# The last two projection tiles in halves: second halves between attention's first steps, and one selection tile later

## The chip, the cores and the metric

The kernel runs on one core of one Trainium2 chip. The metric is the device time of one execution in microseconds (us). TensorE (PE) multiplies matrices and transposes, VectorE (DVE), ScalarE (ACT) and GpSimd (POOL) compute on tiles, and SyncE (SP) issues the transfers between DRAM and on-chip memory (SBUF). Matmul results land in eight banks of PSUM.

## The reference

One decoder block on 1024 tokens of width 1024. Eight heads of width 64 attend with an index-based selection of 256 keys (DSA), and eight with a forgetting bias (FoX). Cut to what matters:

```
h = modulate(rms_norm(x), sh1, sc1)
proj = h @ w_in                      # q, k, v of both head groups, index heads, forget gates
q_d, k_d, v_d, iq, ik, iw, q_f, k_f, v_f, f_logit = split(proj)
score = sum_h(relu(iq . ik) * iw)    # per query and key, causal
keys = top_k(score, 256)             # the selection of the DSA heads
o_d = softmax(q_d . k_d over keys) @ v_d
o_f = softmax(q_f . k_f + cum_q - cum_k, causal) @ v_f
x = x + g1 * (concat(rms_norm(o_d), rms_norm(o_f)) @ w_out)
x = x + g2 * swiglu(modulate(rms_norm(x), sh2, sc2))
out = rms_norm(x)
```

## The kernel before

Every engine has its own program, written out in order. They meet in semaphores (`wait_ge`, `then_inc`), and an engine that waits holds up all that stands behind the wait in its program.

**Projections.** `w_in` is taken in seven chunks of columns (NC = 7), each in eight tiles of 128 tokens (TT = 8). A tile adds eight steps of k, each with three matmuls (function `three`, lines 2151 to 2153, since a number is kept as a high and a low part), into one PSUM bank: 24 matmuls of 128x512. The banks 0 to 3 are used in turn. ScalarE empties a tile into `stage` (line 1132), and SyncE stores it into DRAM (line 696). Chunk 6, the last, holds V of the DSA heads.

**Selection.** While the projections run, VectorE and ScalarE find for each tile of queries the threshold of the 256th key. `choose` (lines 1724 to 1747) then turns one tile of scores into a mask in eight steps on VectorE, for the tiles 2 to 7 in order. `advance(CHOICE_EARLY)` does the first five tiles, 2 to 6, before attention, and `CHOICE_LATE` puts the eight steps of tile 7 one by one behind steps of heads 1 and 2. Masks are used from head 8 on.

**Attention.** It runs over 128 steps s = 8 x head + tile. At step s TensorE computes the logits (lines 2330 and 2332), two matmuls for each group of up to 512 keys, into the banks 0 and 1 or 2 and 3. VectorE adds the bias and takes the maximum (`biased`, line 1798), ScalarE exponentiates (line 1251), TensorE transposes the probabilities two steps later (line 2311, banks 4 and 5), ScalarE copies them out, and the products with V (line 2357, banks 6 and 7) begin at step 12. FoX heads come first (0 to 7), then DSA heads.

**The head loop.** Heads need K and Q rows, which were stored in DRAM. There is one pair of buffers, `Qd` and `Kd`. GpSimd's `prepare(hd)` (lines 923 to 931) waits for their arrival, makes high and low parts in five instructions, and ends with line 931. SyncE's `load_qk(hd)` issues four fetches (line 663), and waits first until the head before is prepared:

```
def load_qk(hd):
    if hd >= 1:
        sp.wait_ge(k_lo, hd)
        sp.wait_ge(q_lo, hd)
```

After the last store of the projections SyncE's program reads, line 730 on:

```
for i in range(2):
    sp.wait_ge(stage_out[i], 16 * (NC - 1) * TT // 2)
sp.wait_ge(pj_pe, NC * TT)
sp.wait_ge(marks_free, 1)
load_values(0)
load_values(1)
for hd in range(2 * NH - 2):
    ...
    load_qk(hd + 2)
```

`stage_out` counts the landed stores of all tiles, `load_values` fetches V for a pair of heads (line 654, two fetches each). Heads 0 and 1 are fetched earlier, among the stores. On GpSimd `prepare(0)` runs under the projections, and `prepare(1)` waits for the end of all tiles (`pj_pe`), because its results lie where the low part of h was.

## Time and profile before

| | |
|---|---|
| time, median of 3 runs | 1386.51 us (1385.52 to 1388.21) |
| the profiled execution | 1386.66 us, of it span 1384.7 us |
| TensorE busy | 1313.3 us, 95% of the span |
| VectorE, ScalarE, GpSimd busy | 72%, 50%, 61% |
| projections' last tile emptied by ScalarE | 370.07 us after the span's start |
| heads 6 and 8 begin on TensorE | 454.87 and 485.94 us |

Times in the rows below are microseconds from the span's start. Each timeline row gives start, duration, engine, line of the program, instruction, the tile written and the tile read. A bracket gives the idle time of the engine before it and what ended it ("issue" where the profile shows nothing that it waited for). Matmuls overlap, so the distance of two starts is what one costs.

### The profile page before, as it was taken

Reading aid. Unit: us, or ns where it says so; the run is one execution under the profiler, and the core shown is the slowest. Engines: PE = TensorE matmul, PEld = TensorE weight load, DVE = VectorE, ACT = ScalarE, POOL = GpSimd, SP = SyncE. Lnnn points to the kernel's source line nnn. Section 1 sums busy time; section 2 is a strip of 40 time slices with the busy share of each in tenths; the row PEclk is TensorE's granted clock in tenths of the full one; section 3 lists DMA queues with packets and bytes.
Section 4 is the critical chain, followed back from the end, with each engine's and each line's share of the span. In section 5 each row is a group of like instructions: output and inputs, shape, how many; then the busy total and the mean of one; then the engine's idle time right before and its main releaser. Section 6 shows DMA issues by size and latency. Waiting matters only on the chain.

```text
span 1384.7 us, 19484 instructions
## 1 busy us (share of the span) xinstructions
PE 1313.3 (95%) x6595; PEld 1074.1 (78%) x6595; DVE 995.2 (72%) x1583; ACT 696.0 (50%) x1396; POOL 848.1 (61%) x552
## 2 busy tenths in 40 slices
PE   1999999999999999899999899999999999999996
PEld 0988778888777677668888788888888888788885
DVE  4563779999866888876569666555556666589998
ACT  6623345563388777773345344333444333454545
POOL 0161403324249745931027899888889984798995
PEclk9799999999999999999999999999999999999998
DMA  9131312342345777605010333233333234998873
GB/s 380 55 97 56 94 52 92 107 124 77 110 113 160 239 221 219 200 32 193 38 45 31 97 120 109 93 107 107 115 114 110 89 122 152 391 352 301 288 249 143
DMA packets 130379, 200.53 MB, mean 145 GB/s; under 512 B 10637, under 2 KB 65093, under 8 KB 129258
## 3 DMA queue, kind: packets, MB, share of 16 engines
q1 hardware_dynamic: 130282, 199.30, 43.1%
q8 instruction: 53, 0.87, 0.3%
q14 instruction: 44, 0.36, 0.1%
HBM read 156.99 MB, written 42.27 MB: 144 GB/s over the span
## 4 chain that ended last, share of the span: by engine, by line
PE 78%; DVE 9%; issue 4%; ACT 3%; DMA 3%; POOL 2%; SPq 1%; ACTq 0%; DVEq 0%; POOLq 0%
PE PS L2151 20%; PE PS L2152 20%; PE PS L2153 20%; PE PS L2357 4%; PE PS L2311 4%; DVE AS L2017 3%; PE PS L2330 2%; DMA ada<-in_ada_w_dram 2%; DVE BS L2022 1%; PE PS L2332 1%; POOL WSf L1012 1%; PE PS L2335 1%; ACT LP L1251 1%; DVE PS L2074 1%; POOL WS L1024 1%
## 5 line engine op out<-in xcount | busy, mean ns | idle before, releaser
L1330 ACT CAST WS<-WSf 128x512 fp32r<-128x512 f32 x110 | 68.5, 622 | 203.6 <-POOL WSf L1012 202.9
L1024 POOL TENSOR_TENSOR WS<-WSf,WS 128x512 fp32r<-128x512 f32 x109 | 163.4, 1506 | 4.4 <-ACT WS L1330 4.4
L1012 POOL TENSOR_TENSOR WSf<-rawg 128x512 f32<-128x512 f32 x55 | 78.5, 1428 | 117.0 <-PE PS L2153 112.5
L2151 PE MATMUL PS<-yh,WS 128*128 128x512 f32 (+2 forms) x360 | 140.4, 390 | 1.5 <-DVE yl L1931 1.5
L2152 PE MATMUL PS<-yl,WS 128*128 128x512 f32 (+2 forms) x360 | 140.1, 389 | 0.0
L2153 PE MATMUL PS<-yh,WS 128*128 128x512 f32 (+2 forms) x360 | 140.0, 389 | 0.0
L2151 PE MATMUL PS<-BS,AS 128*128 128x512 f32 x308 | 121.0, 393 | 4.6 <-DVE BS L2022 3.4
L2017 DVE TENSOR_TENSOR AS<-rawa,AS 128x512 fp32r<-128x512 f32 x77 | 104.9, 1382 | 23.0 <-ACT AS L1389 22.8
L2153 PE MATMUL PS<-BS,AS 128*128 128x512 f32 x308 | 120.5, 391 | 0.0
L2152 PE MATMUL PS<-BS,AS 128*128 128x512 f32 x308 | 120.4, 391 | 0.0
L1251 ACT ACTIVATE LP<-LP,nmin 128x128 f32<-128x128 f32 (+7 forms) x128 | 100.2, 783 | 23.3 <-DVE nmin L1798 22.0
L1043 POOL TENSOR_TENSOR BS<-rawb,BS 128x512 fp32r<-128x512 f32 x57 | 90.6, 1595 | 27.9 <-ACT BS L1393 27.7
L2151 PE MATMUL PS<-XH,WS 128*128 128x512 f32 x264 | 103.5, 392 | 4.0 <-POOL WS L1024 4.0
L1640 DVE TENSOR_SCALAR_CACHE_REDUCE marks_c<-sel,bis 128x640 f32<-128x640 f32 (+4 forms) x135 | 103.3, 818 | 0.6
L2153 PE MATMUL PS<-XH,WS 128*128 128x512 f32 x264 | 103.2, 391 | 0.0
L2152 PE MATMUL PS<-XL,WS 128*128 128x512 f32 x264 | 103.2, 391 | 0.0
L2311 PE MATMUL PS<-ident,LP 128*128 128x128 f32 x576 | 90.4, 282 | 6.8 <-ACT PTb L1241 2.7
L1036 POOL TENSOR_TENSOR rawb<-rawb 128x512 f32<-128x512 f32 x55 | 90.3, 1651 | 7.9 <-DMA rawb<-in_w_down_dram 7.9
L1157 ACT ACTIVATE PS<-sel,bis 128x896 f32<-128x896 f32 x64 | 67.6, 1056 | 50.3 <-DVE bis L1695 35.2
L2311 PEld LDWEIGHTS PS<-ident,LP 128*128 128x128 f32 x576 | 66.2, 143 | 29.0 <-ACT PTb L1241 8.7
L1012 POOL TENSOR_TENSOR WSf<-rawu 128x512 f32<-128x512 f32 x55 | 84.5, 1537 | 3.4 <-PE PS L2153 2.5
L1389 ACT CAST AS<-rawa 128x512 fp32r<-128x512 f32 x77 | 47.9, 622 | 75.0 <-PE PS L2153 64.2
(337 smaller groups left out, 3820.4 us busy)
## 6 DMA issues: line engine op xcount, KB each, us to landing
rawb<-in_w_down_dram SPq DMA_DIRECT2D x132, 256.0 KB, 4.5
rawa<-gu_scratch SPq DMA_DIRECT2D x77, 256.0 KB, 4.5
gu_scratch<-GS SPq DMA_DIRECT2D x55, 256.0 KB, 4.5
raw<-in_w_in_dram SPq DMA_DIRECT2D x24, 512.0 KB, 3.9
rawg<-in_w_gate_dram SPq DMA_DIRECT2D x22, 512.0 KB, 4.3
rawu<-in_w_up_dram SPq DMA_DIRECT2D x22, 512.0 KB, 4.3
ada<-in_ada_w_dram SPq DMA_DIRECT2D x8, 1024.0 KB, 15.3
qk_scratch<-stage SPq DMA_DIRECT2D x32, 256.0 KB, 2.1
```

The costliest lines, as they stand in the source:

```text
L1012: pool.tensor_tensor(WSf[m % N_SLOT][:], left(i, mat, a), left(i, mat, b), ALU.add if sign > 0 else ALU.subtract).then_inc(ws_sum, 1)
L1024: pool.tensor_tensor(lo, WSf[m % N_SLOT][:] if b else left(i, mat, a), hi.bitcast(F32), ALU.subtract).then_inc(ws_ready, 1)
L1036: pool.tensor_tensor(r[:, 0, :], r[:, 0, :], r[:, 1, :], ALU.add if RIGHT[DOWN[m // PAIRS]][2] > 0 else ALU.subtract).then_inc(gb_sum, 1)
L1043: pool.tensor_tensor(b[:, 1, :], rawb[m % DOWN_RAW_B][:, 0, :], b[:, 0, :].bitcast(F32), ALU.subtract).then_inc(gb_lo, 1)
L1251: act.activation(LP[:, u % 3, 0:n], LP[:, u % 3, 0:n], ACT.Exp, bias=nmin[:, u:u + 1], scale=-1.0, accum_out=sums[:, u:u + 1]).then_inc(ex ...
L1330: act.copy(WS[m % N_SLOT][:, 0], src).then_inc(ws_hi, 1)
L1640: did(dve.tensor_scalar(marks[0][:, n_tk % 2, 0:P * (t + 1)], view(t), limit, 0.0, op, ALU.add, accum_out=col(0, t)))
L2017: dve.tensor_tensor(AS[m % DOWN_SLOTS][:, 1, :], rawa[m % DOWN_RAW_A][:], AS[m % DOWN_SLOTS][:, 0, :].bitcast(F32), ALU.subtract).then_inc ...
L2151: pe.matmul(dst, left[0], right[0], start=first, stop=False)
L2152: pe.matmul(dst, left[0], right[1], start=False, stop=False)
L2153: return pe.matmul(dst, left[1], right[0], start=False, stop=last)
L2311: last = pe.transpose(dst[:, i * P:(i + 1) * P], src, ident[:])
```

## The change

The tiles 6 and 7 of chunk 6 (`HELD_TILES`) go into the banks 6 and 7. At their place in the projections TensorE does only the first half, k = 0 to 3, and counts it in `held_half`. The rest goes in four pieces of six matmuls behind the steps 0 to 3 of attention (`HELD_AT`). VectorE and not ScalarE copies the two tiles to `stage`, behind the bias steps 3 and 5 (`HELD_EVAC`). ScalarE makes a dummy exponential ahead of emptying tile 5. GpSimd's `prepare(1)` waits for `held_half`. `advance(CHOICE_EARLY)` does four tiles of selection, and the sixteen steps of tiles 6 and 7 stand behind steps of heads 1, 2 and 3.

```diff
-CHOICE_TILES = ((), (1, 2, 6, 7), (1, 2, 6, 7))
+CHOICE_TILES = ((), (1, 2, 3, 6, 7), (0, 1, 2, 5, 6, 7), (1, 2, 3, 6, 7))
...
-CHOICE_EARLY = 5 * CHOICE_OPS
+CHOICE_EARLY = 4 * CHOICE_OPS
+HELD_TILES = (TT - 2, TT - 1)
+HELD_AT = {0: (TT - 2, 4), 1: (TT - 2, 6), 2: (TT - 1, 4), 3: (TT - 1, 6)}
+HELD_EVAC = {3: TT - 2, 5: TT - 1}
...
+def proj_bank(ch, t):
+
+    return t if ch == NC - 1 and t in HELD_TILES else (TT * ch + t) % 4
...
             pool.wait_ge(cumT_ok, 2)
             prepare(0)
+            pool.wait_ge(held_half, len(HELD_TILES))
+            prepare(1)
             pool.wait_ge(pj_pe, NC * TT)
-            prepare(1)
...
                 elif step[0] == "tile":
+                    if step[1] == NC - 1 and step[2] in HELD_TILES:
+                        continue
+                    if step[1:] == (NC - 1, HELD_TILES[0] - 1):
+                        act.activation(junk[:, 0:1], ones[:, 0:1], ACT.Exp)
                     if step[3:] != (0,):
                         evac_tile(step[1], step[2])
...
-            dve.wait_ge(pj_pe, NC * TT)
+            def evac_held(t):
+                n = (NC - 2) * TT + t
+                dve.wait_ge(pj_pe, (NC - 1) * TT + t + 1)
+                dve.wait_ge(stage_out[n % 2], 16 * (n // 2))
+                dve.tensor_copy(stage[:, n % 2, :], PS[:, proj_bank(NC - 1, t), :]).then_inc(pj_ev, 1)
+
+            dve.wait_ge(held_half, len(HELD_TILES))
             for s in range(UNITS):
                 hd, t = divmod(s, TT)
                 biased(s)
+                if s in HELD_EVAC:
+                    evac_held(HELD_EVAC[s])
...
+                held = ch == NC - 1 and t in HELD_TILES
+                dst = PS[:, proj_bank(ch, t), 0:w]
+                if held and rows_of.start == 0:
+                    pe.wait_ge(sign_cnt, len(SIGN_TILES) * BISECT)
...
+                elif held and rows_of.stop == KT // 2:
+                    last.then_inc(held_half, 1)
...
-                    tile(*step[1:])
+                    if step[1] == NC - 1 and step[2] in HELD_TILES:
+                        tile(*step[1:], part=0)
+                    else:
+                        tile(*step[1:])
...
-                    pe.wait_ge(pj_ev, NC * TT - 2 * (1 - u))
+                    pe.wait_ge(pj_ev, NC * TT - len(HELD_TILES))
...
+                        if p == 0 and g == 0:
+                            pe.wait_ge(pj_ev, NC * TT)
...
                 values(s, 2)
+                if s in HELD_AT:
+                    t, k = HELD_AT[s]
+                    tile(NC - 1, t, rows_of=range(k, k + 2))
```

TensorE's order at the end of the projections, before the change (`wh`, `hh` and `hl` are weights and input of the projections, `KA` and `QT`, `CK` and `CQ` the two parts of the logits, and `LP` the probabilities that are transposed):

```order
L2151 MATMUL PS<-wh,hh 128x512
L2152 MATMUL PS<-wh,hh 128x512
L2153 MATMUL PS<-wh,hl 128x512
L2330 MATMUL PS<-KA,QT 128x128
L2332 MATMUL PS<-CK,CQ 128x128
L2330 MATMUL PS<-KA,QT 128x256
L2332 MATMUL PS<-CK,CQ 128x256
L2330 MATMUL PS<-KA,QT 128x384
L2332 MATMUL PS<-CK,CQ 128x384
L2311 MATMUL PS<-ident,LP 128x128
```

TensorE's order at the same place in the changed kernel, from the last matmul before attention:

```order
L2175 MATMUL PS<-wh,hl 128x512
L2361 MATMUL PS<-KA,QT 128x128
L2363 MATMUL PS<-CK,CQ 128x128
L2173 MATMUL PS<-wh,hh 128x512
L2174 MATMUL PS<-wh,hh 128x512
L2175 MATMUL PS<-wh,hl 128x512
L2173 MATMUL PS<-wh,hh 128x512
L2174 MATMUL PS<-wh,hh 128x512
L2175 MATMUL PS<-wh,hl 128x512
L2361 MATMUL PS<-KA,QT 128x256
L2363 MATMUL PS<-CK,CQ 128x256
```

Six projection matmuls now stand between the logits of step 0 and those of step 1; the same holds behind the steps 1, 2 and 3.

VectorE's order where selection ends and attention begins, before the change (`sel` is the scores and mask, `marks_c` a scratch tile, and the rows with `strip` and `nmin` are the bias steps 0 and 1):

```order
L1735 SCALAR_TENSOR_TENSOR marks_c<-marks_c 128x896
L1739 SCALAR_TENSOR_TENSOR marks_c<-marks_c,bis 128x896
L1743 SCALAR_TENSOR_TENSOR sel<-sel,bis,marks_c 128x896
L1747 TENSOR_SCALAR sel<-sel 128x896
L1798 ISA LP,nmin<-PS,strip 128x128
L1798 ISA nmin 128x1
L1798 ISA LP,nmin<-PS,strip 128x256
L1798 ISA nmin 128x1
```

VectorE's order in the changed kernel, from the bias step 3 to the bias step 6:

```order
L1812 ISA LP,nmin<-PS,strip 128x512
L1812 ISA nmin 128x1
L1864 COPY stage<-PS 128x512
L1812 ISA LP,nmin<-PS,strip 128x640
L1812 ISA nmin 128x1
L1812 ISA LP,nmin<-PS,strip 128x768
L1812 ISA nmin 128x1
L1864 COPY stage<-PS 128x512
L1812 ISA LP,nmin<-PS,strip 128x896
```

The steps of tile 6 (128x896) are gone from the place ahead of attention, and two copies into `stage` stand behind the bias steps 3 and 5. SyncE's and GpSimd's instructions stand in the same order as before.

## Rows read from the trace of the kernel before

**Rows 1.** The page: busy time of the engines, and the chain by engine

```profile
PE 1313.3 (95%) x6595; PEld 1074.1 (78%) x6595; DVE 995.2 (72%) x1583; ACT 696.0 (50%) x1396; POOL 848.1 (61%) x552
...
PE 78%; DVE 9%; issue 4%; ACT 3%; DMA 3%; POOL 2%; SPq 1%; ACTq 0%; DVEq 0%; POOLq 0%
```

**Rows 2.** ScalarE's timeline at the end of the projections: start us, us, instruction

```profile
364.63 0.60 ACT L1132 ACTIVATE stage<-PS 128x512 f32<-128x512 f32 x1 [4.84 <-PE PS L2153]
370.07 0.60 ACT L1132 ACTIVATE stage<-PS 128x512 f32<-128x512 f32 x1 [4.84 <-PE PS L2153]
370.69 1.28 ACT L1251 ACT_TABLE_LOAD   x1
```

**Rows 3.** TensorE's timeline at attention's first steps; in brackets the idle time before

```profile
369.88 0.22 PE L2330 MATMUL PS<-KA,QT 128*128 128x128 f32 x1
...
370.73 0.39 PE L2330 MATMUL PS<-KA,QT 128*128 128x256 f32 x1 [0.52 <-ACT stage L1132]
...
372.53 0.33 PE L2311 MATMUL PS<-ident,LP 128*128 128x128 f32 x1 [0.95 <-ACT LP L1251]
372.62 0.48 PE L2330 MATMUL PS<-KA,QT 128*128 128x512 f32 x1
...
395.01 0.33 PE L2330 MATMUL PS<-KA,QT 128*128 128x128 f32 x1
```

**Rows 4.** SyncE's queue after the projections (what it issues)

```profile
372.75 2.02 SPq L654 DMA_DIRECT2D Vn<-v_scratch  x4
378.03 1.09 SPq L663 DMA_DIRECT2D Qd<-qk_scratch  x2
...
392.94 1.11 SPq L663 DMA_DIRECT2D Qd<-qk_scratch  x2
```

**Rows 5.** GpSimd's timeline: in the preparation of heads 1, 2, 3 and 6

```profile
375.58 2.37 POOL L931 TENSOR_TENSOR QT<-Qd,QT 64x1024 fp32r<-64x1024 f32 x1
...
385.05 1.04 POOL L923 CAST QT<-Qd 128x1024 fp32r<-128x1024 f32 x1 [5.01 <-DMA Kd<-qk_scratch]
...
399.79 2.04 POOL L923 CAST QT<-Qd 128x1024 fp32r<-128x1024 f32 x1 [6.92 <-DMA Kd<-qk_scratch]
...
451.55 3.22 POOL L931 TENSOR_TENSOR QT<-Qd,QT 64x1024 fp32r<-64x1024 f32 x1
```

**Rows 6.** GpSimd's waits from 385 to 490 us: us in total, times, longest

```profile
POOL QT L923 <- DMA Kd<-qk_scratch: 27.2, 6, 7.0
```

**Rows 7.** SyncE's waits in the same stretch

```profile
SPq L660 <- POOL QT L931: 62.7, 7, 12.5
```

**Rows 8.** TensorE's timeline where heads 6 and 8 begin

```profile
454.87 0.30 PE L2330 MATMUL PS<-KA,QT 128*128 128x128 f32 x1 [2.74 <-issue]
...
485.94 0.30 PE L2330 MATMUL PS<-KA,QT 128*128 128x128 f32 x1 [0.81 <-issue]
```

**Rows 9.** Windows: engines' busy time, granted clock, DMA share, GB/s

```profile
373.50:378.50 5.00, 5.00 (x26) 4.54 (x25) 2.72 (x7) 3.90 (x11) 4.86 (x3) 0.66 0.71 210
394.00:398.50 4.50, 4.50 (x40) 3.40 (x37) 2.98 (x8) 3.56 (x9) 0.00 (x0) 1.00 0.94 235
```

**Rows 10.** DMA issues from 372 to 376 us: KB each, us to landing

```profile
Vn<-v_scratch SPq DMA_DIRECT2D x4, 256.0 KB, 3.5
```

**Rows 11.** DMA issues from 425.6 to 427 us, behind a head's rows

```profile
Vn<-v_scratch SPq DMA_DIRECT2D x2, 256.0 KB, 5.3
```

**Rows 12.** VectorE's timeline: selection of tile 6, one bias step, two later selection steps

```profile
361.34 0.68 DVE L1724 TENSOR_SCALAR sel<-sel,bis 128x896 f32<-128x896 f32 x1
...
368.45 0.63 DVE L1747 TENSOR_SCALAR sel<-sel 128x896 f32<-128x896 f32 x1
...
376.67 0.96 DVE L1798 CUSTOM_DVE_ANT_0 LP<-PS,strip 128x768 f32<-128x768 f32 x1 [1.11 <-PE PS L2332]
...
399.65 1.28 DVE L1739 SCALAR_TENSOR_TENSOR marks_d<-marks_d,bis 128x1024 f32<-128x1024 f32 x1
...
406.44 3.23 DVE L1743 SCALAR_TENSOR_TENSOR sel<-sel,bis,marks_d 128x1024 f32<-128x1024 f32 x1
```

More of the change, by code:

```diff
@@ L477, in build @@
         pj_ev = sem("pj_ev")
+        held_half = sem("held_half")
         ir_st = sem("ir_st")
@@ L2188, in tile @@
                     pe.wait_ge(mod1_ok, 2)
-                if q >= 4 and rows_of.start == 0:
+                held = ch == NC - 1 and t in HELD_TILES
+                dst = PS[:, proj_bank(ch, t), 0:w]
+                if held and rows_of.start == 0:
+                    pe.wait_ge(sign_cnt, len(SIGN_TILES) * BISECT)
+                elif q >= 4 and rows_of.start == 0:
                     pe.wait_ge(pj_ev, q - 3)
@@ L2201, in tile @@
                         rows = slice(half * BANK, (half + 1) * BANK)
-                        last = three(PS[:, q % 4, 0:w], (hi[:, cols], lo[:, cols]), (hh[:, k, rows], hl[:, k, rows]),
+                        last = three(dst, (hi[:, cols], lo[:, cols]), (hh[:, k, rows], hl[:, k, rows]),
                                      k == 0, k == KT - 1)
@@ L2206, in tile @@
                     rows = slice(t * P, (t + 1) * P)
-                    last = three(PS[:, q % 4, 0:w], (hh[:, k, rows], hl[:, k, rows]), (hi[:, cols], lo[:, cols]),
+                    last = three(dst, (hh[:, k, rows], hl[:, k, rows]), (hi[:, cols], lo[:, cols]),
                                  k == 0, k == KT - 1)
```

## Prediction

> **What bounds the kernel now.** I read the page first. TensorE is busy for 95% of the span and holds 78% of the chain that ended last [rows 1], so a change can gain only by taking time out of TensorE's path. The place to look at is the handover from the projections to attention. The timelines show what is spent there: after the last projection matmul TensorE starts attention at 369.88, stands 0.52 us until ScalarE has emptied the last tile, and 0.95 us until the first exponential is there [rows 3], which has a 1.28 us table load ahead of it [rows 2]. In the following 5 us the granted clock averages 0.66 [rows 9], so part of them ran at 1.2 GHz instead of 2.4.
>
> Then I asked whether a TensorE that is earlier there stays earlier. It does not have to. Each head needs its K and Q rows: SyncE fetches them from DRAM, GpSimd prepares them, and SyncE may fetch the next head's rows only when that is done, as there is one pair of buffers. SyncE issued head 2's fetch at 378.03 [rows 4], right when GpSimd ended head 1 (375.58 + 2.37 = 377.95 [rows 5]). GpSimd began on head 2 at 385.05, and the next fetch went out at 392.94 [rows 4, 5]. This loop has no slack: from 385 to 490 us GpSimd waited for the fetched rows six times [rows 6] and SyncE for GpSimd seven times [rows 7]. It takes 14.9 us in this round, and from 378.03 to the start of head 8 at 485.94 [rows 4, 8] 107.9 us for seven heads, 15.4 us each. TensorE alone goes faster: from head 2 (395.01 [rows 3]) to where it stands ready for head 6 (454.87 - 2.74 = 452.13 [rows 8]) it takes 57.1 us for four heads, 14.3 each. So it catches up with the loop. At head 6 it stands 2.74 us, until GpSimd has ended (451.55 + 3.22 = 454.77 [rows 5]), and at head 8 another 0.81 [rows 8]. **Up to head 8 the loop sets the time, and the loop hangs on the moment at which head 2's fetch is issued.**
>
> **The change, part by part.**
>
> *Half tiles moved on TensorE.* One projection tile of 24 matmuls takes 370.07 - 364.63 = 5.44 us [rows 2]. Two second halves are 24 matmuls too, so attention starts 5.44 us earlier, at 364.44. The matmuls themselves stay. They go where TensorE stood or waited for ScalarE, together with the 0.52 us of waiting for the last tile. The table load, now made by a dummy exponential before tile 5 is emptied, leaves the path: ScalarE waits 4.84 us for each tile [rows 2], which hides 1.28. That would be worth up to 0.52 + 0.95 + the slow clock's share, 0.34 x 5 = 1.7, some 3.2 us in all, if nothing else bound.
>
> *Selection of tile 6 on VectorE.* Its eight steps run from 361.34 to 368.45 + 0.63 = 369.08 [rows 12], 7.7 us. They would have been in the way of a bias step at 364.8, and now go into heads 1 to 3. There they cost TensorE nothing as long as what they delay is less than its standing at head 6, 2.74 us and more; without that cover they would cost up to 7.7 us.
>
> *Head 1's preparation on GpSimd.* It now waits for the two half tiles only, which end 5.44 us earlier, so it ends at 377.95 - 5.44 = 372.5. This looks like a gain for the loop, but nothing follows from it, because of the next part.
>
> *The last two stores on SyncE's queue.* Nothing in SyncE's program changes, but it is in order: store of tile 6, store of tile 7, wait for both to land, four fetches of V, and only then head 2's K and Q. Tile 7 used to be emptied at 370.07 + 0.60 = 370.67 [rows 2]. Now VectorE does it after the bias step of step 5. TensorE must do before it: four pieces, 5.44; the logits of steps 0 to 5, which are 2 x 128 x (1 + ... + 6) = 5376 columns at the projections' rate of 5.44 / (24 x 512) us, 2.38; and six transposes at about 0.1 (372.53 to 372.62 [rows 3]), 0.6. That is 8.4 us from 364.44, so 372.9. The bias step takes 0.96 [rows 12] with some 0.3 before it, and the copy is bounded by nothing and 0.6 (ScalarE's for the same tile [rows 2]); with 0.6 it ends at 374.8. From the emptied tile to the first fetch of V it took 372.75 - 370.67 = 2.08 us, and the four issues 2.02 [rows 2, 4]. So head 2's fetch goes out at 374.8 + 2.08 + 2.02 + 0.04 = 378.9 instead of 378.03: **about 0.9 us later**, though everything before it is earlier. Each wait of TensorE in its first five steps adds to this one to one.
>
> *K and Q behind V.* Before, V's 1 MB was done when K and Q were asked for (landing 3.5 us after issue [rows 10]). Now they are asked for directly behind it. If the transfers simply overlap, the fetch takes as long as before: added cost 0. If they queue, V's bytes flow until 3.5 us after its last issue at about 378.4, to 381.9, and then K and Q need 4.5 us more (the 394.0 to 398.5 window, DMA 94% busy [rows 9]) and about 1.3 to be noticed (398.5 to 399.79 [rows 5, 9]): 387.7, against 378.9 + 7.0 = 385.9. Added cost 1.8. A sign of queueing is that V issued directly behind K and Q takes 5.3 instead of 3.5 us [rows 10, 11]. I take 1.4, nearer to the upper end. The Trainium skill, page "DMA: Bandwidth & Descriptors", section "Queues, rings and completion order", says that each DMA engine consumes the descriptors of a ring in order; by that rule the cost is the full 1.8, and the sum below is 0.4 higher. Rows 10 and 11 agree with it.
>
> *GpSimd against VectorE.* GpSimd's cast of head 3 at 399.79 took 2.04 us instead of 1.04 [rows 5]; VectorE's selection step of 1.28 us had begun at 399.65 [rows 12]. Another such step took 3.23 us at 406.44 [rows 12]. The two delay each other, and each meeting can add up to 1 us to the loop. The change shifts the phases and puts eight more such steps into heads 1 to 3, so the loop may lose one meeting (-1.0) and get up to two (+2.0). I take 0. The Trainium skill, page "SBUF — State Buffer", section "Who interferes with whom", speaks against the change here: such VectorE steps and GpSimd's take a port in turn, for a whole instruction. By that rule each new meeting costs, and the two above agree with it in size.
>
> **Sum.** Loop later by 0.9 + 1.4 + 0 = 2.3 us at head 8. Head 2 begins at about 387.3 + (392.94 - 385.05) = 395.2, hardly later than before, after a stand of some 3 us; TensorE may then lose again what the slow clock took, 1.7 us, and reaches head 6 before the loop does. From head 8 on TensorE leads the time again, so the 2.3 stay. The profiled execution took 1386.66 us, 0.15 above the median of three runs; median: 1386.51 + 2.3 = **1388.8 us**. That is slower by 0.17%; a difference below 0.2%, 2.8 us, can't be told from none here.
>
> **The rivals.**
> - *The loop holds* (my forecast, 0.70). With the fetch alone +0.9 and one meeting lost, -0.1; with full queueing and two meetings, 0.9 + 1.8 + 2.0 = +4.7. Time 1386.4 to 1391.2, nearly symmetric about 1388.8. For it: rows 4 to 8.
> - *VectorE becomes the bound* (0.10). Its 7.7 us more in heads 1 to 3 hold up TensorE, by way of bias steps, for more than the 2.74 + 2.3 - 0.2 - 1.7 = 3.1 us that are there before head 6. If half of it, 3.9, and two steps lengthened by 2 us like that of 406.44 come through, 7.9 - 3.1 = 4.8 us are added to the 2.3: 1393.6. Against it: the steps stand behind bias steps and are short beside a head's 14 us.
> - *The ramp's gain is kept* (0.12). The 3.2 us are saved, and the loop is not late. That asks for a fetch of head 2 issued by 375, three us earlier than before; it decides from a tile 7 emptied by 370.8. Then 1386.5 - 3.2 = 1383.3. Against it stands that the copy of tile 7 has 8.4 us of TensorE before it, which start at 364.44. A smaller form is that K and Q do not hang behind V's issues and meetings are lost.
> - *Nothing moves* (0.08): the fetch goes out at 378.0, since steps 0 to 5 are shorter than I make them: 1386.5.
>
> **How the numbers follow.** The median is slower by over 2.8 us (above 1389.3) in 0.38 of the first case (0.27) and all of the second: 0.37. It is faster by as much (below 1383.7) in some 0.08 of the third and nowhere else: 0.08. The rest is 0.55. The range 1385.6 to 1391.4 takes in the bounds of the first case and the last one, and leaves out the second and most of the third.
>
> **What the profile would show.** The first attention matmul at 364.4; no table load before the first exponential; tile 7 copied by VectorE at about 374.2; V's fetches at 376.9 and head 2's at 378.9; GpSimd's cast of head 2 at 387.3 instead of 385.05; TensorE standing some 3 us before head 2; heads 6 and 8 beginning 2.3 us later than 454.87 and 485.94. I am wrong if head 2's fetch goes out before 378, if the six waits of GpSimd are gone, or if TensorE no longer stands at head 6.

## The result, and the profile after

The changed kernel took 1398.05 us in the median of four runs (1395.71 to 1398.89), the kernel before 1387.36 (1385.52 to 1389.32): ratio 1.0073, 95% interval 1.0052 to 1.0095. It is slower by 0.73%, about four times what was forecast, and outside the range. The profiled execution took 1397.99 us, 11.3 more than the one of before.

What was forecast up to the fetch of head 2 is there. ScalarE's timeline has the table load behind the last tile but one that it empties, not ahead of the first exponential [rows 2]:

```profile
352.60 0.60 ACT L1142 ACTIVATE stage<-PS 128x512 f32<-128x512 f32 x1 [4.84 <-PE PS L2175]
353.22 1.28 ACT L1202 ACT_TABLE_LOAD   x1
...
364.14 0.40 ACT L1265 ACTIVATE LP<-LP,nmin 128x128 f32<-128x128 f32 x1 [5.50 <-DVE nmin L1812]
```

VectorE's timeline has the two held tiles' copies, at 369.78 and 373.36, 0.69 us each:

```profile
369.78 0.69 DVE L1864 COPY stage<-PS 128x512 f32<-128x512 f32 x1
...
373.36 0.69 DVE L1864 COPY stage<-PS 128x512 f32<-128x512 f32 x1
```

SyncE's queue issues head 2's fetch (line 672) at 378.96 instead of 378.03 [rows 4], directly behind the four fetches of V, and the next one at 397.63 instead of 392.94:

```profile
370.50 3.90 SPq L705 DMA_DIRECT2D v_scratch<-stage  x2
376.12 2.74 SPq L663 DMA_DIRECT2D Vn<-v_scratch  x4
378.96 1.10 SPq L672 DMA_DIRECT2D Qd<-qk_scratch  x2
380.10 1.24 SPq L672 DMA_DIRECT2D Kd<-qk_scratch  x2
381.38 1.24 SPq L750 DMA_DIRECT2D RX<-qk_scratch  x2
...
397.63 1.11 SPq L672 DMA_DIRECT2D Qd<-qk_scratch  x2
```

TensorE's timeline starts attention at 363.28. It stands 6.87 us before head 2, and still 2.65 at head 6 and 0.83 at head 8, which start 9.1 and 9.2 us later than before [rows 8]:

```profile
363.28 0.22 PE L2361 MATMUL PS<-KA,QT 128*128 128x128 f32 x1
...
397.66 0.45 PE L2361 MATMUL PS<-KA,QT 128*128 128x128 f32 x1 [6.87 <-POOL QT L940]
...
424.20 0.51 PE L2361 MATMUL PS<-KA,QT 128*128 128x512 f32 x1 [1.29 <-DVE nmin L1812]
...
463.99 0.30 PE L2361 MATMUL PS<-KA,QT 128*128 128x128 f32 x1 [2.65 <-issue]
...
495.14 0.30 PE L2361 MATMUL PS<-KA,QT 128*128 128x128 f32 x1 [0.83 <-issue]
```

So nearly all of the time is lost between 378 and 495 us, in the loop of SyncE and GpSimd. Its legs, worked out from the two timelines: "fetch" runs from the issue of a head's Q rows to GpSimd's first cast of them (in heads 5 to 7 it holds parts of GpSimd's rotation of RX too), "prepare" from there to the end of its last instruction. The next issue follows 0.07 us later.

```
head      before: fetch, prepare    after: fetch, prepare    loop later by (with the 0.93 at its start)
2                 7.02  7.82               9.14  9.46              4.7
3                 6.85  8.80               7.62  8.15              4.8
4                 6.66  7.84               6.90 10.78              8.0
5                 7.27  8.68               8.60  8.67              9.3
6                 6.86  8.65               6.69  8.62              9.1
7                 6.79  9.37               6.98  9.20              9.1
8                 6.93  7.83               7.01  7.81              9.2
```

Three places hold nearly all of it: the fetch of head 2 (+2.1), and the preparations of heads 2 and 4 (+1.6 and +2.9) with the rotation ahead of head 5's (6.01 instead of 4.70 us). GpSimd's timeline shows what happened in them. An undisturbed cast takes 1.04 us, whether of 128 or of 64 partitions; here one takes 2.77, one 3.04 and one 2.02:

```profile
388.10 1.05 POOL L932 CAST QT<-Qd 128x1024 fp32r<-128x1024 f32 x1 [14.62 <-DMA Kd<-qk_scratch]
389.09 1.05 POOL L933 CAST KA<-Kd 128x1024 fp32r<-128x1024 f32 x1
390.07 2.77 POOL L935 CAST CQ<-Qd 64x1024 fp32r<-64x1024 f32 x1
...
420.37 1.04 POOL L932 CAST QT<-Qd 128x1024 fp32r<-128x1024 f32 x1 [6.98 <-DMA Kd<-qk_scratch]
421.35 3.04 POOL L933 CAST KA<-Kd 128x1024 fp32r<-128x1024 f32 x1
424.34 2.02 POOL L935 CAST CQ<-Qd 64x1024 fp32r<-64x1024 f32 x1
...
431.23 6.01 POOL L949 TENSOR_TENSOR RT<-RX,turnF 128x1024 f32<-128x1024 f32 x2
```

VectorE's timeline has a selection step beside each of them:

```profile
389.80 2.22 DVE L1749 TENSOR_TENSOR_SCAN marks_d<-marks_d 128x896 f32<-128x896 f32 x1
...
421.28 2.28 DVE L1749 TENSOR_TENSOR_SCAN marks_d<-marks_d 128x1024 f32<-128x1024 f32 x1
424.06 1.40 DVE L1753 SCALAR_TENSOR_TENSOR marks_d<-marks_d,bis 128x1024 f32<-128x1024 f32 x1
```

The scan of tile 7 has just begun when GpSimd reaches its second cast. It ends at 423.56, and the cast ends 0.83 us behind it, as if it had stood until then. The next cast ends 0.90 us behind the following step. Undisturbed, no other step is as long as the scan (2.02 us on 896 columns, 2.29 on 1024 in the kernel before), and the prediction's bound of one microsecond for a meeting came from a shorter step [rows 5, 12]. The Trainium skill, page "SBUF — State Buffer", section "Who interferes with whom", has a VectorE instruction with two inputs in SBUF contend with a GpSimd instruction that reads SBUF, and the one that comes second blocked for the whole of the other; these rows agree.

From the start of head 8 on TensorE to the end the two profiles differ by another 2.4 us (901.2 us instead of 898.8). That is not laid to the change: over all profiles of this study this stretch lies between 893.8 and 901.7.

The slow clock of attention's first steps [rows 9] is gone: windows of the changed kernel give a granted clock of 1.00 from 366 to 396 us. Behind the stand before head 2 it comes back. The columns are the length, the busy time of TensorE (its matmuls, its weight loads), VectorE, ScalarE and GpSimd, the granted clock, the DMA share and GB/s:

```profile
366.00:396.00 30.00, 22.74 (x148) 18.05 (x147) 16.83 (x36) 21.21 (x53) 15.16 (x10) 1.00 0.45 123
...
398.00:402.00 4.00, 4.00 (x19) 2.73 (x18) 2.86 (x6) 1.93 (x5) 0.00 (x0) 0.50 0.77 196
402.00:404.00 2.00, 2.00 (x13) 1.63 (x11) 0.00 (x0) 0.84 (x2) 0.00 (x0) 0.78 0.63 141
```

### The profile page after: what moved, and what is told of

The parts are those of the page before. It is cut to its first block, busy times and chain, and to the rows that moved or that the text cites. A ratio compares the mean times of both kernels' runs of the same rounds, so it can differ in the third digit from the quotient of the medians.

```text
span 1396.3 us, 19486 instructions
## 1 busy us (share of the span) xinstructions
PE 1315.9 (94%) x6595; PEld 1076.5 (77%) x6595; DVE 1007.5 (72%) x1585; ACT 695.4 (50%) x1395; POOL 845.8 (61%) x552
## 4 chain that ended last, share of the span: by engine, by line
PE 56%; DVE 5%; issue 4%; ACT 2%; POOL 2%; DMA 1%; SPq 0%; ACTq 0%; DVEq 0%; POOLq 0%
PE PS L2173 15%; PE PS L2175 15%; PE PS L2174 15%; PE PS L2390 4%; PE PS L2342 4%; PE PS L2361 2%; POOL WSf L1022 1%; DVE AS L2039 1%; PE PS L2366 1%; PE PS L2363 1%; DVE LP L1812 1%; POOL WS L1034 1%; PE PS L2407 0%; DMA rawa<-gu_scratch 0%; PE PS L2372 0%
## 5 line engine op out<-in xcount | busy, mean ns | idle before, releaser
L2039 DVE TENSOR_TENSOR AS<-rawa,AS 128x512 fp32r<-128x512 f32 x77 | 100.7, 1323 | 25.7 <-ACT AS L1403 25.5
L2361 PE MATMUL PS<-KA,QT 128*128 128x512 f32 (+1 forms) x192 | 78.2, 407 | 13.6 <-POOL QT L940 6.9
```

The costliest lines, as they stand in the source:

```text
L2039: dve.tensor_tensor(AS[m % DOWN_SLOTS][:, 1, :], rawa[m % DOWN_RAW_A][:], AS[m % DOWN_SLOTS][:, 0, :].bitcast(F32), ALU.subtract).then_inc ...
L2361: pe.matmul(dst, q, KA[i][:, b:b + w], start=True, stop=False)
```

## The experiments

Each was timed in turn with the kernel before on the same chip. All were made from the changed kernel, except where "from the kernel before" is said. "Head 8" is the end of its preparation in the profile (before 485.85, changed 495.04), "ratio" the time against the kernel before. A tenth of a per cent is 1.4 us. Medians of different rows can come from different chips, so they are compared by the ratios.

```
                                     median us   ratio [95% interval]         head 8
selection alone (from before)          1391.57   1.0027 [1.0002, 1.0053]      490.33
held tiles alone                       1397.25   1.0063 [1.0040, 1.0087]      497.49
fetch first                            1386.68   0.9994 [0.9967, 1.0020]      487.55
V then K and Q (from before)           1391.90   1.0028 [1.0001, 1.0055]      491.67
one column                             1390.30   1.0007 [0.9989, 1.0025]      489.42
fetch first, one column                1382.65   0.9961 [0.9942, 0.9981]      480.96
fetch first, RX later                  1386.37   0.9994 [0.9970, 1.0018]      484.01
the same, steps placed                 1387.98   0.9994 [0.9970, 1.0018]      484.76
scan and two-input steps short         1392.45   1.0028 [1.0011, 1.0046]      491.06
multiplications short                  1395.08   1.0048 [1.0030, 1.0066]      494.87
changed kernel again                   1397.05   1.0067 [1.0044, 1.0091]      495.55
fetch first, selection of before       1388.88   0.9993 [0.9977, 1.0010]      485.56
```

**The selection alone**, from the kernel before.

```diff
-CHOICE_TILES = ((), (1, 2, 6, 7), (1, 2, 6, 7))
+CHOICE_TILES = ((), (1, 2, 3, 6, 7), (0, 1, 2, 5, 6, 7), (1, 2, 3, 6, 7))
-CHOICE_EARLY = 5 * CHOICE_OPS
+CHOICE_EARLY = 4 * CHOICE_OPS
```

> The kernel before with the change's selection alone: four tiles ahead of attention, the sixteen steps of tiles 6 and 7 behind steps of heads 1 to 3; no held tiles. Theory (GpSimd's preparation loop sets the time, and selection steps on VectorE that fall into a preparation lengthen it): head 2's fetch goes out at 378.0 as before; the scan of head 3's part and the step behind it fall into the preparation of head 4, which takes 10 to 11 us instead of 7.8; head 8 begins 2 to 4 us later than 485.94; time 2 to 4 us above the kernel before. Rival (the ramp and the fetch order alone make the loss, selection costs nothing): within 1 us of the kernel before. Rival (VectorE holds up TensorE's bias steps): slower too, but with GpSimd's preparations at 7.8 us and TensorE's waits for VectorE grown.

The time is 3.7 us above the kernel before (0.3 to 7.4), and head 8 is 4.5 us later, although head 2's fetch goes out 2.5 us earlier, at 375.51, since the projections end earlier in this profile (why was not found). From that issue to the end of head 8's preparation the loop takes 114.8 us instead of 107.8. 2.2 of the 7.0 us are the preparation of head 4, which takes 10.01, with the end of tile 7's scan and the step after it beside its first two casts. So the new steps are paid for without any held tile.

Another 1.8 us are the fetch of head 2, which takes 8.79 instead of 7.02. V is not the reason: it is issued 5.3 us ahead of the fetch, as in the kernel before [rows 4].

```profile
370.19 2.02 SPq L654 DMA_DIRECT2D Vn<-v_scratch  x4
...
375.51 1.09 SPq L663 DMA_DIRECT2D Qd<-qk_scratch  x2
```

Where V stands directly ahead the Q rows land late, and here they do not. The DMA issues of head 2's rows (KB each, median us to landing), in the kernel before, with the selection alone, and in the changed kernel:

```profile
Qd<-qk_scratch SPq DMA_DIRECT2D x2, 256.0 KB, 3.9
Kd<-qk_scratch SPq DMA_DIRECT2D x2, 256.0 KB, 4.9
```

```profile
Qd<-qk_scratch SPq DMA_DIRECT2D x2, 256.0 KB, 3.9
Kd<-qk_scratch SPq DMA_DIRECT2D x2, 256.0 KB, 5.9
```

```profile
Qd<-qk_scratch SPq DMA_DIRECT2D x2, 256.0 KB, 5.2
Kd<-qk_scratch SPq DMA_DIRECT2D x2, 256.0 KB, 6.6
```

In all seven profiles with V directly ahead of head 2's fetch the Q rows take 5.1 to 5.8 us, in the seven others 3.6 to 4.0. The K rows behind them vary by more, and why is open.

**The held tiles alone**: the same two lines, set back in the changed kernel.

> The changed kernel with the selection of the kernel before: five tiles ahead of attention, eight steps in heads 1 and 2. The bias of step 0 then waits for VectorE until about 369. Theory: tile 7 is copied at about 376.7, head 2's fetch goes out at 380.8 (2.8 us later than 378.03), behind V, which adds 1.6 to 2.1; with 0 to 1 us of meetings the loop is 4.4 to 6 us late at head 8, time 4 to 6 us above the kernel before. Rival (selection steps are the whole loss): time within 1 us of the kernel before. Rival (the ramp's gain shows once selection is out of the way): 2 to 3 us below the kernel before.

As slow as the whole change, but by another way. Tile 6's selection now stands between TensorE's first logits and VectorE's first bias step (370.37), and head 1's preparation, brought forward to 363.77, falls beside it and takes 11.00 us. TensorE waits 3.8 us for that step, and its granted clock is 0.50 from 370 to 376, while it works on the second halves that the stores wait for. Head 2's fetch goes out at 385.05, 7 us later than before and 4 later than I expected, and takes 10.28. The time is 8.7 us above the kernel before, more than the 4 to 6 of the theory. The costs of the two parts do not add up: each shifts where the other's work falls.

**Fetch first**: head 2's K and Q are issued ahead of the held tiles' stores, when head 1's preparation is done.

```diff
                     q = TT * (ch - 1) + t
+                    if (ch, t) == (NC - 1, HELD_TILES[0]):
+                        load_qk(2)
                     sp.wait_ge(pj_ev, TT * ch + t + 1)
...
-                load_qk(hd + 2)
+                if hd >= 1:
+                    load_qk(hd + 2)
```

> The changed kernel with head 2's K and Q fetch issued ahead of the stores of the two held tiles. Theory: the fetch goes out at 372.6 instead of 378.96, lands in 7 us, GpSimd ends head 2 at 387 to 388 instead of 397.56, and TensorE does not stand at head 2. The loop then leads by some 6 us over the kernel before, loses 2 to 5 in meetings with selection, and head 6 begins at 450 to 454 against 454.87 before: time 1 to 4 us below the kernel before, 11 to 14 below the changed one. Rival (the late fetch is not what costs; VectorE's load is): TensorE gains at head 2 but is held up in heads 1 to 3, and the time stays more than 5 us above the kernel before.

SyncE's queue and GpSimd's timeline:

```profile
371.81 1.08 SPq L672 DMA_DIRECT2D Qd<-qk_scratch  x2
372.93 1.24 SPq L672 DMA_DIRECT2D Kd<-qk_scratch  x2
374.21 1.06 SPq L707 DMA_DIRECT2D v_scratch<-stage  x2
380.18 2.02 SPq L663 DMA_DIRECT2D Vn<-v_scratch  x4
382.24 1.21 SPq L752 DMA_DIRECT2D RX<-qk_scratch  x2
...
387.26 1.11 SPq L672 DMA_DIRECT2D Qd<-qk_scratch  x2
```

```profile
379.14 1.30 POOL L935 CAST QT<-Qd 128x1024 fp32r<-128x1024 f32 x1 [5.32 <-DMA Kd<-qk_scratch]
...
396.91 1.04 POOL L935 CAST QT<-Qd 128x1024 fp32r<-128x1024 f32 x1 [9.72 <-DMA Kd<-qk_scratch]
...
414.33 3.10 POOL L938 CAST CQ<-Qd 64x1024 fp32r<-64x1024 f32 x1
417.39 3.34 POOL L941 TENSOR_TENSOR CK<-Kd,KA 64x1024 fp32r<-64x1024 f32 x1
```

The fetch is 7.15 us earlier than in the changed kernel and takes 7.33 us with V behind it and not ahead. The time falls back to that of the kernel before, and not to the 1 to 4 us below it that I expected: head 8 is 7.5 us earlier than in the changed kernel and still 1.7 later than before. The queue is now in front of head 3's fetch, which has V and RX ahead of it and takes 9.65, and head 4's preparation meets scan and next step again (11.14). V itself is now late, issued at 380.18 instead of 372.75, and TensorE's timeline has a wait for it:

```profile
384.01 0.40 PE L2393 MATMUL PS<-PTa,Vn 128*64 128x256 f32 x1 [1.20 <-DMA Vn<-v_scratch]
```

**V, then K and Q**, from the kernel before: V is only asked for when head 1 is prepared, so that head 2's fetch stands directly behind it.

```diff
             sp.wait_ge(marks_free, 1)
+            sp.wait_ge(k_lo, 2)
+            sp.wait_ge(q_lo, 2)
             load_values(0)
```

> The kernel before, with the four fetches of V held back until head 1 is prepared, so that they go out right ahead of head 2's K and Q; nothing else. It measures the disputed delay by itself and whether it is passed on. Theory: V issued at 378.05 to 380.1, K and Q at 380.1 (2.1 later); behind V they take 8.8 to 9.1 us instead of 7.0; the loop is 3.9 to 4.2 us late, passed on one to one: head 8 at about 490, time 3.5 to 4.5 us above the kernel before. Rival (transfers overlap): 2.1 us. Rival (the delay is absorbed by later slack): within 1 us.

The fetch goes out at 379.26, 1.2 us later than before, and takes 9.51 instead of 7.02. That is the queue without held tiles or selection: 2.5 us, of which the Q rows show 1.7 (they land after 5.6 us instead of 3.9). Head 8 is 5.8 us later. The ratio gives 3.9 us (0.1 to 7.6), as the theory has it. By the time alone the rival of an absorbed delay, within 1 us, is not excluded; head 8 in the profile speaks against it. One of the ten times, 3368 us, is far outside the others (1387.5 to 1397.9); the ratio leaves it out, and the median without it is 1390.23.

**One column**: of the selection of tiles 6 and 7 every step but the count works on one column. Masks of these two tiles are left out by this.

```diff
                     v, n = view(t), P * (t + 1)
+                    if t >= FIRST_TOPK + CHOICE_EARLY // CHOICE_OPS:
+                        v, n = v[:, 0:1], 1
```

> The changed kernel with the selection steps of tiles 6 and 7 (except their counts) done on one column instead of 896 and 1024, so the masks of these two tiles are not those of the reference; every wait and transfer stays. It takes the meetings of VectorE and GpSimd away and leaves the late and queued fetch. Theory (fetch late and queued 3.0 us, meetings 6 us): preparations of heads 2 and 4 take 7.8 us each instead of 9.46 and 10.78, head 5's rotation 4.7 instead of 6.0; head 8 begins about 6 us earlier than in the changed kernel; time 3 to 5 us above the kernel before. Rival (the fetch alone makes the loss): as the changed kernel, +9 to +11.

The preparations of heads 2, 3 and 4 take 7.73, 7.82 and 7.82 us, the rotation 4.70 as before. Head 8 is 5.6 us earlier than in the changed kernel, as expected. The time is 1.0 us above the kernel before (-1.5 to 3.5), some 9 us less than with the change and less than the 3 to 5 that I expected. Of the 3.6 us that head 8 is still later than before, 2.5 are the fetch: issued at 378.65, it takes 8.86. Other preparations shift too: head 6's takes 9.63 instead of 8.65.

**Fetch first and one column** together (the same two edits, the same masks left out).

> The same one-column steps, and head 2's K and Q fetched ahead of the two last stores: both costs taken away (masks of tiles 6 and 7 not those of the reference). Theory: head 2's fetch goes out at 371.8, the loop leads the kernel before by 6 us and loses only what head 3's fetch loses behind V and the rotation's rows (2.7 us); head 8 begins 3 to 5 us before 485.94; time 3 to 5 us below the kernel before. Rival (something else in the ramp costs): above -1 us.

The preparation of head 8 ends 4.9 us earlier than before, and the time is 0.39% less, 5.4 us (2.6 to 8.1). TensorE does not stand before head 6, which begins at 453.16 (before 454.87 [rows 8]), nor before head 8, which begins at 483.30, 2.6 us earlier than before and 2.3 behind its preparation. So TensorE and not the loop sets the time here; it had waited 1.64 us for V at 384.8, and its granted clock was 0.65 and 0.50 from 386 to 390. With both costs taken out a gain is left. The prediction's third rival asked for a fetch issued by 375 and gave it 3.2 us; here it is issued at 372.21. But the kernel with the fetch first and the selection whole issues it at 371.81 and keeps nothing: the early fetch is needed, and not enough.

**Fetch first, RX later**: the fetch of RX moves behind head 3's K and Q.

```diff
-                if hd == 1:
-                    sp.wait_ge(qk_pe, TT)
-                    for i in range(2):
-                        sp.dma_start(RX[i][:], rope_rows(i)).then_inc(rx_in, 16)
...
                 if hd >= 1:
                     load_qk(hd + 2)
+                if hd == 1:
+                    for i in range(2):
+                        sp.dma_start(RX[i][:], rope_rows(i)).then_inc(rx_in, 16)
```

> The changed kernel with head 2's fetch first, and the two fetches for the rotation (RX, 1 MB) moved behind head 3's K and Q. Full selection. Theory (queueing: head 3's K and Q took 9.65 us behind V and RX): that fetch takes 7 to 7.5 us, head 8 begins 1.5 to 2.5 us earlier than with the fetch alone moved, unless the meetings change; time 2 to 3 us below the kernel before. Rival (a meeting on VectorE and not the queue made 9.65): the fetch stays above 9 us and the time within 1 us of the kernel before.

Fetches of heads 2 and 3 take 6.76 and 7.03 us: the queue is gone (head 3's took 9.65 without this edit). Some of that is given back in meetings: the loop now reaches the selection at other places, and the preparations of heads 2, 3 and 4 take 8.19, 9.10 and 11.09. Head 8's preparation ends 1.8 us earlier than before, and TensorE begins the head 0.7 earlier, at 485.21. The time does not differ from the kernel before, where I expected 2 to 3 us less.

**The same with the steps placed by hand** in slots between preparations, some two or three together.

```diff
-CHOICE_LATE = {TT * hd + t: 1 for hd, tiles in enumerate(CHOICE_TILES) for t in tiles}
+CHOICE_LATE = {13: 1, 14: 3, 15: 1, 21: 2, 22: 2, 23: 2, 28: 2, 29: 1, 30: 2}
```

> The kernel of the run before, with the sixteen selection steps put behind those bias steps that fall into GpSimd's waits for a fetch (steps 13 to 15, 21 to 23, 28 to 30, several at once) instead of one by one. Theory: the preparations of heads 2 to 4 take 7.8 to 8.2 us each, VectorE holds up TensorE by 1 to 2 us in bursts, head 8 begins 4 to 6 us before 485.94, time 3 to 6 us below the kernel before: a version that beats both. Rival (bursts on VectorE cost TensorE what the meetings cost the loop): no faster than the run before.

Preparations of heads 2 to 4 are free of meetings (7.78, 7.82, 7.81), but the next ones are not: 9.57 us go by before head 5's (its fetch and the rotation), head 7's takes 10.88. And now VectorE holds up TensorE, which was the other side of the argument. VectorE's and TensorE's timelines:

```profile
414.94 1.60 DVE L1748 TENSOR_SCALAR marks_d<-sel,bis 128x1024 f32<-128x1024 f32 x1
416.57 4.33 DVE L1751 TENSOR_TENSOR_SCAN marks_d<-marks_d 128x1024 f32<-128x1024 f32 x1
420.82 0.93 DVE L1814 CUSTOM_DVE_ANT_0 LP<-PS,strip 128x768 f32<-128x768 f32 x1
```

```profile
421.81 0.79 PE L2363 MATMUL PS<-KA,QT 128*128 128x512 f32 x1 [3.94 <-DVE nmin L1814]
```

The scan, 2.28 us in the changed kernel, took 4.33 beside GpSimd's rotation, which had begun at 416.06 and took 7.00 instead of 4.70. A bias step waited behind the scan, and TensorE 3.94 us for that. It begins head 8 at 487.10, 2.3 us behind the preparation and 1.2 later than before. The rival holds: no faster than the run before.

**Which steps do it.** In the first of two kernels the scan and both two-input steps of tiles 6 and 7 work on one column (m is 1 for them, and the last multiplication is then by 0), in the second the first and last multiplication; either leaves out those tiles' masks.

```diff
+                    m = 1 if t >= FIRST_TOPK + CHOICE_EARLY // CHOICE_OPS else n
...
-                    did(dve.tensor_tensor_scan(marks[0][:, 1, 0:n], marks[0][:, 0, 0:n], marks[0][:, 0, 0:n], 0.0, ALU.add,
+                    did(dve.tensor_tensor_scan(marks[0][:, 1, 0:m], marks[0][:, 0, 0:m], marks[0][:, 0, 0:m], 0.0, ALU.add,
```

> The changed kernel; of the selection of tiles 6 and 7 the scan and the two steps with two inputs in SBUF (scalar_tensor_tensor) work on one column, so these two tiles' masks are not the reference's; the four steps of tensor_scalar form and the count stay whole. Theory A (the loop loses its 6 us to meetings of the scan and of the two-input steps with GpSimd's preparation): preparations of heads 2 to 5 return to 7.8 to 8.2 us where they took 9.5 and 10.8, the scan at head 4's preparation is gone, and head 8 begins near 489, some 5 to 6 us earlier than in the changed kernel; time near 1390 to 1392. Rival B (the meetings that cost are those of the tensor_scalar steps, as the port rule for copies and tensor_scalar would have it): preparation of head 4 stays at 10 us or more, head 8 begins at 493 or later, time near 1396.

```diff
-                    did(dve.tensor_scalar(v, v, col(5, t), None, ALU.mult))
+                    did(dve.tensor_scalar(v[:, 0:m], v[:, 0:m], col(5, t), None, ALU.mult))
...
-                    dve.tensor_scalar(v, v, BIG, None, ALU.mult).then_inc(tk_done, 1)
+                    dve.tensor_scalar(v[:, 0:m], v[:, 0:m], BIG, None, ALU.mult).then_inc(tk_done, 1)
```

> The changed kernel; of the selection of tiles 6 and 7 the first and the last multiplication (tensor_scalar) work on one column, so these two tiles' masks are not the reference's; scan, two-input steps, count and comparison stay whole. Theory A: the meetings with the scan stay, so the preparation of head 4 takes 10 us or more (it may shift by some us to another head, since VectorE reaches its steps a little earlier), and head 8 begins within 2 us of 495; time within 3 us of the changed kernel. Rival B: preparations return to about 8 us, head 8 near 489 to 490.

With the scan short, head 4's preparation is whole again on GpSimd's timeline:

```profile
419.95 1.04 POOL L932 CAST QT<-Qd 128x1024 fp32r<-128x1024 f32 x1 [6.79 <-DMA Kd<-qk_scratch]
420.93 1.04 POOL L933 CAST KA<-Kd 128x1024 fp32r<-128x1024 f32 x1
421.92 1.03 POOL L935 CAST CQ<-Qd 64x1024 fp32r<-64x1024 f32 x1
422.92 2.39 POOL L938 TENSOR_TENSOR CK<-Kd,KA 64x1024 fp32r<-64x1024 f32 x1
```

Preparations of heads 2 and 4 take 7.72 and 7.82 us. Head 8 comes out 4.0 us earlier than in the changed kernel instead of the 5 to 6 expected, because head 2's fetch took 11.48 us this time; the preparations of heads 2 and 4 and the rotation alone give 5.6. With the multiplications short these two preparations stay at 9.45 and 10.75, with head 8 at 494.87. The multiplications are not free: against the changed kernel on the same chip head 3's preparation takes 7.81 us instead of 8.14 and the rotation 5.58 instead of 6.02. So the scan and the two-input steps make nearly all of the loss, and the multiplications some 0.8 us. The scan and the two-input steps were not taken apart; the rows above show both kinds.

**The changed kernel again**, on the same chip as these two.

> The changed kernel once more, on the chip of the other three, for their comparison. Theory A (order of the instructions and durations decide which preparation meets which step): the same meetings as in its first profile, preparations of heads 2 and 4 of 9.5 and 10.8 us, head 8 at 495 within 1 us, ratio to the kernel before 1.005 to 1.0095. Rival (the meetings fall by chance from run to run): head 8 moves by 2 us or more and the ratio leaves that interval.

Preparations of 9.53 and 10.75 us at heads 2 and 4, head 8 at 495.55: the meetings fall in the same places in both profiles (and at 9.45 and 10.75 us with the multiplications short), as they would if order and durations fix them, and not by chance from run to run.

**Fetch first with the selection of before**: the fetch order from above, the selection's two lines set back.

> The changed kernel with the selection steps where they stood before (five tiles' worth ahead of attention, the rest at eight places in heads 1 and 2) and with head 2's fetch ahead of the held tiles' stores. Theory A (loop): head 1's preparation now meets the selection steps of tile 6 and ends about 375, as in the version with the held tiles alone, so head 2's fetch goes out at about 375 instead of 385.05 there; it does not queue behind V; head 8 begins 7 to 10 us earlier than in that version (497.6), at 488 to 490, and the time is 1387 to 1391. Rival (TensorE's path through the late bias steps of steps 0 to 5 costs by itself, not by way of the loop): head 8 begins at 493 or later and the time stays near 1396.

No difference from the kernel before. Head 1's preparation takes 10.97 us (beside tile 6's selection) and ends at 373.72, still 4.2 us earlier than before; the fetch takes 7.01. The gain goes at head 3: its fetch stands behind V and RX (8.94), its preparation beside the scan (10.77), and head 8 ends at 485.56. The held tiles by themselves cost nothing here once the fetch does not hang on them, and gain nothing. The rival of a cost on TensorE's own path is out, though TensorE waits 3.8 us there for a first bias step.

## Why the prediction was wrong

- *TensorE starts 5.44 us earlier, table load off the path*: right (see the first rows above; 6.6 us earlier in the profile, 1.2 of it not from the change as worked out).
- *The loop sets the time up to head 8, and what it is late stays*: right. Head 6 and head 8 are 9.1 and 9.2 us later, and in all twelve versions the shift of head 8 and that of the time by the ratio agree within 3 us; the kernel before with V held back shows it without any part of the change (in its profile; its time has a wide interval). In three of the versions with the fetch first TensorE reaches head 8 later than the loop does and sets the time itself.
- *Head 2's fetch 0.9 us later, since it hangs behind two stores and V*: right, 0.93. The chain behind it (copy, store, V) was right too; the profiled execution of the changed kernel starts attention 1.2 us earlier than I worked out (363.28 against 364.44), and VectorE's second copy ended at 374.05 instead of 374.8, but the four issues of V took 2.74 us instead of 2.02, so that the two errors cancelled.
- *K and Q behind V, 1.4 us*: mechanism right, size too small. It measured 2.1 here and 2.5 with V alone in the way. Over all versions the fetch takes 8.8 to 11.5 us with V directly ahead and 6.8 to 7.8 without, but for the 8.79 with the selection alone, which shows that not all of it is the queue. Full queueing, 1.8 in my working, was no upper bound.
- *GpSimd against VectorE, 0*: **this is the step that failed.** "Each meeting can add up to 1 us to the loop", and "the loop may lose one meeting (-1.0) and get up to two (+2.0). I take 0." Heads 2, 4 and the rotation ahead of head 5 paid 1.6, 2.9 and 1.3 us, less 0.65 saved at head 3: 5.2 in all. I had priced a meeting by one cast that met a short step [rows 5, 12], and had not looked at the scan, the longest of the eight steps. In the kernel before it runs from 397.00 to 399.29 and so ends half a microsecond ahead of head 3's preparation; now it falls twice into preparations. And I had taken gains and losses as about as likely, although more steps beside the same loop mean more meetings on average.
- *TensorE catches up*: right, with little to spare. It reached head 2 6.87 us before the loop, not some 3, since the loop was later. From there to where it is ready for head 6 (463.99 - 2.65 = 461.34) it takes 63.7 us instead of 57.1: the slow clock behind that stand, forecast at 1.7 us, measured some 2.6 (an estimate from the clock of 0.50 and 0.78 between 397.7 and 404), and the waits for VectorE and another stretch of slow clock (0.68 from 425 to 430) came on top. 2.65 us of standing were left.

With the sizes measured in the profile the sum reads 0.9 + 2.1 + 5.2 + 0.8 (a slower fetch at head 3) + 0.2 = 9.2 at head 8, and 1386.51 + 9.2 = 1395.7; the four runs of the changed kernel lie between 1395.71 and 1398.89. Their median, 1398.05, is 2.4 above the sum, as much as the stretch from the start of head 8 on differs between the two profiles (of 1397.99 and 1386.66 us). Of the rivals, VectorE as the bound of TensorE did not hold: TensorE waits for it 1.29 and 0.49 us at head 4 and still stands 2.65 before head 6. Placed in bursts the steps do that. The third rival, the kept gain, did not come, and shows only where both costs are gone and two tiles' masks are left out.

Three things stay open. Why a fetch behind V takes 8.8 us in one kernel and 11.5 in another was not found: the Q rows differ by 0.7 us, the K rows behind them by 1.8 (medians 6.4 and 8.2). Nor was it found why head 3's fetch, with nothing ahead of it, takes 0.8 us longer in the changed kernel. And why the stretch behind head 8 differs by up to 8 us between profiles was not studied. None of the versions that compute the whole result is measurably faster than the kernel before.

## What to carry to other kernels

When a loop of two engines has no slack, ask of a change first when the loop's next transfer is issued and what stands ahead of it in the queue, and only then what the busiest engine saves. Price a possible collision by the longest instruction that can be in the way, not by one collision that a trace happens to show, and count work added beside such a loop as a loss until a run shows otherwise. In this kernel an early start was kept only where the fetch behind it did not depend on work that was put off, and where nothing met the loop on the way.

## What the runs showed of the hardware

- GpSimd's cast of 1.04 us took up to 3.10 beside VectorE's scan of 2.28 us, and the scan itself 4.33 where GpSimd was first. In the two meetings read above the loss is the time that was left of the other's instruction. Whether VectorE's two multiplications of a tile covered 1024 columns or one made no difference to the preparations with the scan in them (9.45 and 10.75 us against 9.53 and 10.75), and 0.3 and 0.4 us to another preparation and the rotation.
- Head 2's 1 MB of K and Q took 6.8 to 7.8 us from issue to use where V was not directly ahead (8.79 once), 8.8 to 11.5 directly behind 1 MB of V. The first half, the Q rows, landed after 3.6 to 4.0 us without V and 5.1 to 5.8 with it, in 14 profiles and without exception. The Trainium skill, page "DMA: Bandwidth & Descriptors", section "Queues, rings and completion order", has descriptors of a ring consumed in order, which agrees in sign; the full delay of 2.1 to 2.5 us is larger than the 1.8 that I worked out from V's landing.
- The kernel before spread from 1380 to 1396 us over the 86 runs beside these versions, and the intervals of the ratios are 0.16 to 0.27% wide to each side, so that smaller differences can't be told from none.
